# Combinations by twos beside q, and the first output operands among the last taps, in a hybrid decoder layer

## The reference

```
h = rms_norm(x, ln_g)
u, g_pool, c_a, c_b, g_conv, q, k, v, g_attn = split(h @ w_in)
y_pool = pool_mixer(u, pool_w, pool_scale)      # trailing means over 2, 4, 8, 16 tokens minus the token
y_conv = silu(layer_norm(causal_depthwise_31(c_a * sigmoid(c_b)) + conv_b)) @ conv_pw
y_attn = attention(q, k, v, sinks)              # 8 heads, 2 kv heads, window 128, ALiBi
y = concat(y_pool * silu(g_pool), y_conv * silu(g_conv), y_attn * silu(g_attn))
out = rms_norm(x + y @ w_out, final_g)
```

## Time and profile before

| what | value |
|---|---|
| median of 3 runs | 1468.28 us (1467.59 to 1469.66) |
| the profiled execution | 1469.99 us |
| its span | 1468.3 us |
| mean granted clock of TensorE | 0.994 |
| busy: TensorE, VectorE, ScalarE, GpSimd | 1424.7, 1136.6, 504.0, 406.7 us |
| DMA | 196.80 MB, 134 GB/s over the span |

### The profile page before, as it was taken

The page is one execution under the profiler, slowest core; times in us unless marked ns, Lnnn a source line. Parts: engine busy times, 40 slices in busy tenths (PEclk is TensorE's granted clock), DMA queues, the critical chain, the costliest instruction groups (busy, mean ns, idle before and its releaser), DMA issues.

```text
span 1468.3 us, 20261 instructions
## 1 busy us (share of the span) xinstructions
PE 1424.7 (97%) x6992; PEld 1154.8 (79%) x6992; DVE 1136.6 (77%) x2317; ACT 504.0 (34%) x1232; POOL 406.7 (28%) x627
## 2 busy tenths in 40 slices
PE   4999999999999999999999999999999799999997
PEld 4878787777878787878878778787787578888886
DVE  4574848576674738577999988989989978888886
ACT  5444444544444434341112111121112233333332
POOL 5323433332423232120011011010120245555552
PEclk9999999999999999999999999999999899999999
DMA  9116171615241130817033032130425655554531
GB/s 313 60 32 241 58 271 43 257 58 230 99 149 80 57 143 8 307 46 212 1 144 129 16 137 106 43 129 15 173 88 227 272 188 187 158 167 157 161 129 72
DMA packets 77804, 196.80 MB, mean 134 GB/s; under 512 B 14256, under 2 KB 41264, under 8 KB 70064
## 3 DMA queue, kind: packets, MB, share of 16 engines
q1 hardware_dynamic: 63184, 181.40, 32.8%
q10 hardware_dynamic: 14560, 14.68, 3.8%
HBM read 114.27 MB, written 81.79 MB: 134 GB/s over the span
## 4 chain that ended last, share of the span: by engine, by line
PE 80%; DVE 14%; ACT 4%; issue 1%; POOL 1%; DMA 0%; SPq 0%; POOLq 0%; DVEq 0%; ACTq 0%
PE wide L231 12%; PE wide L233 12%; PE wide L232 12%; PE pair L231 10%; PE pair L233 9%; PE pair L232 9%; DVE m_tail L1596 3%; ACT a_rows L672 2%; DVE a_pT L794 2%; DVE a_rows L770 2%; PE turn L233 2%; PE turn L231 2%; PE turn L232 2%; PE pair L1812 2%; PE pair L917 2%; PE wide L946 1%
## 5 line engine op out<-in xcount | busy, mean ns | idle before, releaser
L1596 DVE SCALAR_TENSOR_TENSOR m_tail<-m_tail,m_taps 128x512 f32<-128x512 f32 x480 | 344.4, 762 | 6.5
L231 PE MATMUL pair<-xT,w_hi 128*128 128x512 f32 x640 | 261.2, 408 | 8.2 <-DVE xT L224 4.5
L232 PE MATMUL pair<-xT,w_lo 128*128 128x512 f32 x640 | 251.0, 392 | 0.0
L233 PE MATMUL pair<-xT,w_hi 128*128 128x512 f32 x640 | 250.7, 392 | 0.0
L107 POOL TENSOR_TENSOR pool_carrier<-pool_carrier 128x1 f32<-128x1 f32 x83 | 26.5, 319 | 619.3 <-DVE m_meanvar L1605 402.7
L1395 POOL TENSOR_TENSOR operand_sums<-m_y 128x512 f32<-128x512 f32 x80 | 111.1, 1392 | 180.6 <-PE wide L233 129.1
L231 PEld LDWEIGHTS pair<-xT,w_hi 128*128 128x128 f32 x640 | 121.1, 189 | 33.6 <-DVE a_q L815 7.3
L233 PEld LDWEIGHTS pair<-xT,w_hi 128*128 128x128 f32 x640 | 120.7, 189 | 26.2
L232 PEld LDWEIGHTS pair<-xT,w_lo 128*128 128x128 f32 x640 | 121.2, 189 | 19.9
L231 PE MATMUL wide<-x_first,w_hi 128*128 128x512 f32 x320 | 126.8, 396 | 0.0
L231 PE MATMUL wide<-xT,w_hi 128*128 128x512 f32 x320 | 126.8, 396 | 0.0
(11 more groups left out here) (211 smaller groups left out, 2876.9 us busy)
## 6 DMA issues: line engine op xcount, KB each, us to landing
xT_scratch<-xT SPq DMA_DIRECT2D x16, 2048.0 KB, 15.0
xs<-in_x_dram SPq DMA_DIRECT2D x32, 512.0 KB, 5.2
x_first<-xT_scratch SPq DMA_DIRECT2D x16, 1024.0 KB, 7.4
xT<-xT_scratch SPq DMA_DIRECT2D x16, 1024.0 KB, 9.1
combo_scratch<-stage SPq DMA_DIRECT2D x28, 512.0 KB, 2.8
m_y<-y_scratch ACTq DMA_DIRECT2D x14, 1024.0 KB, 6.7
y_scratch<-y_out SPq DMA_DIRECT2D x8, 1024.0 KB, 5.7
y_scratch<-y_out SPq DMA_DIRECT2D x16, 512.0 KB, 3.1
```

What stands on the lines that cost most here:

```text
L231: nc.tensor.matmul(out, w_hi, x_hi, start=first, stop=False)
L232: nc.tensor.matmul(out, w_lo, x_hi, start=False, stop=False)
L233: return nc.tensor.matmul(out, w_hi, x_lo, start=False, stop=last)
L1596: nc.vector.scalar_tensor_tensor(out=conv[:, i, :], in0=h[:, i, j:j + TB], scalar=taps[:, i, j:j + 1], in1=conv[:, i, :], op0=ALU.mult, op ...
```

## The change

Attention phase: the combinations stand by twos behind q0 (0, 1), q1 (2, 3) and q2 (4, 5), and one (6) behind q3. In each place the sums come first and then the rests. None is left among the score steps. On SP the first four of their stores go ahead of attention's store.

Last mixer block: the five sums of pair 0 are made by VectorE ahead of the first `glu`, with a semaphore of their own (`first_sum`), and no longer by GpSimd. Their hi parts follow behind the first tanh on ScalarE, their rests stand one by one between the first taps. The last six taps and `gate_pool` leave the block.

Output block 0: the first read stands ahead of the held taps, which follow the reads of steps 0 to 4 (2, 1, 1, 1, 1 of them); `gate_pool` follows that of step 5. The convolution's tail moves by one to three steps: turn_conv from 4 to 6, statistics on VectorE and rstd on GpSimd to 7, apply to 9, turn_z to 11, norm_silu to 12, pointwise to 13, gate_conv into output block 1. The rows of x of block 1 use the tail's tiles in another order, and the loads and stores of SP follow them.

The diff, cut to its core:

```diff
@@ attention, sync @@
             store_xT(n)
+            if unit is not None:
+                for i in range(4):
+                    combos.store(sp, unit, i)
             if not isinstance(n, int) or n > 0:
                 store(n - 1)
             if unit is not None:
-                for i in range(STEPS):
+                for i in range(4, STEPS):
                     combos.store(sp, unit, i)
@@ attention, scalar @@
-        def combo(unit, i):
+        def combo(unit, steps):
             if unit is not None:
-                combos.split_hi(act, unit, i)
+                for i in steps:
+                    combos.split_hi(act, unit, i)
...
             q_hi(n, 0)
-            combo(unit, 0)
+            combo(unit, (0, 1))
...
             q_hi(n, 1)
-            combo(unit, 1)
+            combo(unit, (2, 3))
...
             if not final:
                 st.square(act, n + 1)
             q_hi(n, 2)
-            combo(unit, 2)
+            combo(unit, (4, 5))
...
             q_hi(n, 3)
-            combo(unit, 3)
+            combo(unit, (6,))
...
-                if j < 3:
-                    combo(unit, 4 + j)
@@ attention, vector @@
-        def combo(unit, step):
+        def combo(unit, steps):
             if unit is not None:
-                if step < STEPS:
-                    combos.add(dve, unit, step)
-                if step:
-                    combos.split_lo(dve, unit, step - 1)
+                for i in steps:
+                    combos.add(dve, unit, i)
+                for i in steps:
+                    combos.split_lo(dve, unit, i)
...
             make_q_lo(n, 0)
-            combo(unit, 0)
+            combo(unit, (0, 1))
             if not first:
                 output(n - 1, 3, (n, slot("o3")))
...
                 make_q_lo(n, t)
-                combo(unit, t)
+                combo(unit, range(2 * t, min(2 * t + 2, STEPS)))
...
-                combo(unit, 4 + j)
@@ output, sync @@
-            store_pool(NB - 1)
...
-                load_row(1, 1, 3)
+                load_row(1, 1, 0)
+                store_pool(NB - 1)
                 sp.wait_ge(conv_turned, 2 * NB)
-                load_row(1, 1, 0)
-                sp.wait_ge(z_turned, 2 * NB)
                 load_row(1, 1, 1)
-                sp.wait_ge(pw_full, 2 * NB)
-                load_row(1, 1, 2)
+            elif is_block(n, 1):
                 store_conv(NB - 1)
             for q in range(2):
+                if is_block(n, 0) and q == 1:
+                    sp.wait_ge(z_turned, 2 * NB)
+                    load_row(1, 1, 2)
+                    sp.wait_ge(pw_full, 2 * NB)
+                    load_row(1, 1, 3)
@@ mixer and output, gpsimd @@
-                if is_block(n, 0) and at == 4:
+                if is_block(n, 0) and at == 7:
                     layer_norm_rstd(NB - 1)
...
-        for i in range(STEPS):
-            operand_add(0, 0, i)
@@ mixer, scalar @@
                 from_proj(m, r, f"cb{i}", sig[:, i, :], ACT.Tanh, 0.5)
+                if final and i == 0:
+                    for step in range(STEPS):
+                        operand_hi_of(0, 0, step)
...
-            if final:
-                for i in range(STEPS):
-                    operand_hi_of(0, 0, i)
@@ mixer and output, vector @@
+        def first_operand_sums():
+
+            dve.wait_ge(y_loaded[0], 16)
+            dve.wait_ge(proj_full, PROJ * (NB - 1))
+            for i in range(STEPS):
+                if len(LEFT[i]) == 3:
+                    left, op, right = LEFT[i]
+                    nc.vector.tensor_tensor(operand_sums[:, i, 1], y_block(0, left), y_block(0, right), SIGN[op]).then_inc(first_sum, 1)
...
+            if final:
+                first_operand_sums()
             glu(m, r, 0)
...
-                some_taps(m, r, 0, LEAD)
+                for i in range(STEPS if final else 0):
+                    some_taps(m, r, i, i + 1)
+                    operand_lo_of(0, 0, i)
+                some_taps(m, r, STEPS if final else 0, LEAD)
...
-            if final:
-                for i in range(STEPS):
-                    operand_lo_of(0, 0, i)
             some_taps(m, r, GATE_AT, SUMS_AT)
             window_sums(m, r)
-            some_taps(m, r, SUMS_AT, len(TAP_ORDER))
-            gate_pool(m, r)
+            if final:
+                some_taps(m, r, SUMS_AT, HELD_TAPS[0])
+            else:
+                some_taps(m, r, SUMS_AT, len(TAP_ORDER))
+                gate_pool(m, r)
...
+        HELD_TAPS = (56, 58, 59, 60, 61, 62)
...
-                    if at == 4:
+                    if at < 5:
+                        some_taps(NB // 2 - 1, 1, HELD_TAPS[at], HELD_TAPS[at + 1])
+                    elif at == 5:
+                        gate_pool(NB // 2 - 1, 1)
+                    elif at == 7:
                         layer_norm_stats(NB - 1)
-                    elif at == 10:
-                        gate_conv(NB // 2 - 1, 1)
...
+                    if is_block(n, 1) and at == 1:
+                        gate_conv(NB // 2 - 1, 1)
@@ output, tensor @@
-                    if at == 4:
+                    if at == 6:
                         turn_conv(NB - 1)
-                    elif at == 7:
+                    elif at == 11:
                         turn_z(NB - 1)
-                    elif at == 9:
+                    elif at == 13:
                         pointwise(NB - 1)
```

More of the change, by code:

```diff
@@ L1063, in mixer_output_programs @@
     xs = [[sums_flat[:, 0:D], sums_flat[:, D:2 * D], flat(sig), operand_sums[:, STEPS].rearrange("p l k t -> p (l k t)")],
-          [x_rows[:, r] for r in range(SUB)]]
+          [x_rows[:, r] for r in (3, 0, 1, 2)]]
     acc = [proj, [bank[:] for bank in banks.turn + banks.pair]]
@@ L1069, in mixer_output_programs @@
     y_loaded = [sem("y_loaded0"), sem("y_loaded1")]
-    operand_sum, operand_hi, operand_lo = sem("operand_sum"), sem("operand_hi"), sem("operand_lo")
+    first_sum, operand_sum, operand_hi, operand_lo = sem("first_sum"), sem("operand_sum"), sem("operand_hi"), sem("operand_lo")
     gain_loaded = sem("gain_loaded")
@@ L1390, in operand_add @@
                 pool.wait_ge(y_loaded[q], y_uses(n, q))
-                if isinstance(p, int) and p == 0:
-                    pool.wait_ge(proj_full, PROJ * (NB - 1))
-                else:
-                    pool.wait_ge(acc_full, step_of(p - 1, i) + 1)
+                pool.wait_ge(acc_full, step_of(p - 1, i) + 1)
                 nc.gpsimd.tensor_tensor(operand_sums[:, i, 1], y_block(q, left), y_block(q, right), SIGN[op]).then_inc(operand_sum, 1)
@@ L1454, in operand_hi_of @@
             p = 2 * n + q
-            if len(LEFT[i]) == 3:
-                act.wait_ge(operand_sum, sum_of(p, i) + 1)
+            if len(LEFT[i]) == 3 and isinstance(p, int) and p == 0:
+                act.wait_ge(first_sum, sum_of(p, i) + 1)
+            elif len(LEFT[i]) == 3:
+                act.wait_ge(operand_sum, sum_of(p, i) + 1 - sum_of(0, STEPS))
             else:
@@ L1525, in out_body @@
                 if is_block(n, 0):
-                    if at == 5:
+                    if at == 9:
                         layer_norm_apply(NB - 1)
-                    elif at == 8:
+                    elif at == 12:
                         norm_silu(NB - 1)
```

## The result

The changed kernel takes **1491.32 us** (median of 4 runs, 1490.43 to 1492.05), the kernel before 1468.26 beside it: ratio 1.0156, 95% interval 1.0138 to 1.0173. It is 23.1 us slower. The forecast was 10.5 us slower, 1478.8, with a range that ended at 1487: the sign was right, the size was not.

What follows compares the result with a forecast made beforehand. TensorE, busy for 97% of 1468.3 us, was taken as the bound. Border -12.0, attention relief -5.5, stalls +21.6 and clock +6.4 make +10.5 us; added to the median of 1468.28 that gives 1478.8, range 1465 to 1487.

Steps and rivals of the forecast that it cites:

- The border's gain of 12.0: Last mixer and first output block: idle 9.6, slow clock 2.4 and a wait of 0.4 go, less 0.4 new.
- Rival 3: Stalls as forecast, but VectorE falls behind after the border; TensorE waits some 4 us, clock falls again: 1484.4; chance 0.13.
- Two steps of slack each: First output block: statistics, rstd and TensorE's turns behind steps 11 and 13 each have two steps to spare.
- The stalls, 21.6: Attention: TensorE stands 5.4 us at the v projection in each of four bodies, behind late-landing combination stores.
- Rival 1: Attention: small stores pass the large ones, landing about 3 us after issue; nothing stalls: 1450.8; chance 0.12.
- rival 2: Attention: stores wait, but each stall is some 2.5 us shorter: 1462.4, or 1468.8 with the clock's cost; chance 0.15.
- The clock, 6.4: Attention: time lost to half clock behind the four stalls at the v projection, 6.4 us in all.
- The bound of 9.6: Attention: upper bound on the clock's cost behind the four stalls; the lower bound was 0.
- 1.6 for each stall: Attention: clock cost taken behind each of four stalls, from earlier waits that cost 1.7 and 2.4 us.
- Relief in attention, 5.5: Attention: combinations leave the score steps, saving 1.4 us in each of four bodies; bounds 0 and 5.5.
- The border's lower bound of 8: Last mixer and first output block: smallest gain allowed, 8 us, if VectorE falls behind by 4.

Runs made afterwards that it cites:

- border_only: The kernel before with all hunks of the change except those of the attention phase: 1467.74 us, ratio 0.9994.
- border_y_early: border_only with ScalarE issuing the load of y for pair 2 in the last mixer block, some 25 us earlier: 1459.33 us, ratio 0.9935.
- border_combos_behind_y: border_only with SP waiting for the landing of y's load before it issues the last three combinations' loads: 1459.47 us, ratio 0.9943.
- border_fixed: border_y_early with ScalarE's norm_silu of the last block at place 11 instead of 12: 1457.09 us, ratio 0.9924.
- attn_squares_first: The kernel before with the attention part alone, ScalarE's four squares moved ahead of splits 2 and 3: 1469.56 us, ratio 1.0011.
- attn_spread: The kernel before with the attention part alone, combinations 0 and 1 kept as a pair, none behind q1, the others later: 1470.81 us, ratio 1.0012.
- sums_on_gpsimd: border_fixed with the five first sums given back to GpSimd, ahead of its rstd of the last block but one: 1457.13 us, ratio 0.9921.
- attn_xT_behind_four: The kernel before with the attention part alone, stores of combinations 0 to 3 issued ahead of both xT stores: 1488.11 us, ratio 1.0138.

## Why the prediction was wrong, point by point

- **The border's gain of 12.0: the step that failed.** Measured +1.9 in the trace (12.4 less 7.3 of waits and 3.2 of clock), and about 0.5 in border_only. What it worked out for VectorE held: the sums fitted into the gap with 0.23 us over, ten taps took 7.46 (7.3), no hole was left at the fifth step. What it left out is a transfer. It counted the rows of x, the pool store and the conv store on SP's queue and never asked what the earlier window sums let SP issue next: 6 MB of combinations, now beside y's load. The prediction followed the DMAs that the diff moves, and not those that stand behind a wait that the change fulfils earlier. border_y_early and border_combos_behind_y give 8.3 to 8.4 us of it back by moving that transfer alone. Rival 3 saw waits of some 4 us at a bank and a clock cost, for the wrong reason: with y early these waits are gone while VectorE's work is the same.
- **A second, smaller miss at the border.** "Two steps of slack each" was wrong for the pointwise product at step 13, whose input norm_silu comes at 12: a wait of 1.8 us in four traces, with a stretch at half clock behind it in one of them, and 2.2 us between border_y_early and border_fixed. The two were one step apart before, too, without a wait between them. The description of the change has the tail move by one to three steps; these two move by four (8 to 12, 9 to 13).
- **The stalls, 21.6:** 20.7 measured (5.66, 5.30, 5.11, 4.64). Right, and for the reason given: attn_squares_first takes them down by taking the squares out from behind the landing. Rival 1 (small stores pass large ones) and rival 2 (shorter stalls) are out.
- **The clock, 6.4:** 8.3, since TensorE works 16.6 us in the four half-clock stretches. Three of the four stretches last 6.8 us, twice that of the earlier trace rows. The bound of 9.6 held. The term "1.6 for each stall" was too small: 2.1 each.
- **Relief in attention, 5.5:** 4.6 is what is left of 24.4 = 20.7 + 8.3 - 4.6. This is a remainder, not a measurement of its own. attn_spread, with two combinations among the score steps, shows none of it. In attn_squares_first the waits left over take it (4.8 us behind q's rests from 100 to 560, 1.4 before, so some 3.4): its four bodies last 321.6, as before.
- **The sum.** Border 10.1 short, clock 1.9, relief 0.9, stalls -0.9: 12.0 of the 12.5 us by which the forecast missed; the last 0.5 lies between these sums from one trace and the medians. **The range** ended at 1487, from rival 3 with the clock's bound; the border at no gain at all, with attention as forecast, gives 1490.8 and would have had to be in it. The border's lower bound of 8 was drawn from VectorE alone.

## What to carry to other kernels

When a change lets an engine pass a wait earlier, list what that engine's queue issues next, diff or no diff, and with which load it will now share the DMA engines. Here a load in short packets had to be issued ahead of the long ones, or the long ones held back, and either was worth 8.3 us. A store that a later step waits for was here as late as the large stores issued before it on its queue, and moving it ahead only handed the wait to the next one: fill the wait with work that is due anyway, as the squares were here. Pairing side work, or moving it to another engine, is worth what it takes off the bounding engine's path. In attn_spread and in border_fixed against sums_on_gpsimd that was nothing that could be measured.

## What the runs showed of the hardware

- A 1 MB load with packets of about 1 KB landed after 5.6 us with SP's queue held back (border_combos_behind_y) and after 5.7 with a head start of 2.1 us (the kernel before), after 10.2 beside 2 MB of combinations (border_y_early), and after 22.2 beside 6 MB (the changed kernel).
- In a stretch with work on two queues the DMA engines moved as many packets of one as of the other: 294 and 294 from 1166 to 1176 in the changed kernel, with 0.30 and 3.91 MB in them.
- A 0.5 MB store issued behind two 2 MB stores on one queue landed 8.9 us after its issue, where the median of all combination stores had been 2.8.
- The length of one wait of TensorE did not settle whether a lower clock followed. After 2.17 us of idleness 3.4 us at 1.2 of 2.4 GHz followed. After 1.81 us it did in border_y_early and did not in border_combos_behind_y. Three waits of 3.5 us in attn_xT_behind_four were followed by it twice and once not. Around the four waits of 4.6 to 5.7 us in the changed kernel three stretches lasted 6.8 us and one 3.4.
